# An encoder layer's projection: latents' squares and norms on ScalarE, three tiles reordered, the last tile's squares on GpSimd

## The reference

```python
hn = rms_norm(x, p['norm_attn'])
proj = einsum('bsd,de->bse', hn, p['w_in'])
gq, gk, gv, c_q, c_kv, k_pe = split(proj)      # 512, 128, 128, 256, 128, 32 columns
qa, ka = rms_norm per head of gq, gk; then rotated
qb = einsum(rms_norm(c_q), mla_w_uq)           # 8 heads of 64 + 32, each part rms-normed
kvb = einsum(rms_norm(c_kv), mla_w_ukv)        # 8 heads of 64 keys (rms-normed) + 64 values
k_pe = rotated(rms_norm(k_pe))
```

## Time and profile before

| | us |
|---|---|
| median of 3 runs | 1106.34 (1104.49 to 1106.6) |
| the profiled execution | 1105.62 |
| its span, first to last instruction | 1103.8 |
| TensorE busy | 1065.9 (97% of the span) |
| VectorE busy | 882.6 (80%) |
| ScalarE busy | 763.9 (69%) |
| GpSimd busy | 314.1 (28%) |

### The profile page before, as it was taken

How to read it: one execution, slowest core, us unless ns; L and a number is a source line. 1 busy time by engine, 2 the same in 40 slices (tenths; PEclk the granted TensorE clock), 3 DMA queues, 4 the chain that set the end, 5 groups by cost and what they waited for, 6 DMA issues and landing times.

```text
span 1103.8 us, 17117 instructions
## 1 busy us (share of the span) xinstructions
PE 1065.9 (97%) x5835; PEld 915.7 (83%) x5835; DVE 882.6 (80%) x1175; ACT 763.9 (69%) x1033; POOL 314.1 (28%) x346
## 2 busy tenths in 40 slices
PE   8989999999999999999599999999999999999996
PEld 7879978999889988887588888888888888888885
DVE  6787769888998853338898988989889898888982
ACT  8435458887887853443677777877778777787772
POOL 3475467021248602333311101111011110111011
PEclk9999999999999999999699999999999999999998
DMA  8132050010211328541699999999999999999982
GB/s 319 59 110 102 1 193 1 2 39 20 97 39 39 96 76 289 206 177 77 216 420 388 394 389 389 394 410 397 395 388 390 412 397 394 387 392 409 398 304 38
DMA packets 72816, 266.04 MB, mean 241 GB/s; under 512 B 6001, under 2 KB 8268, under 8 KB 72508
## 3 DMA queue, kind: packets, MB, share of 16 engines
q1 hardware_dynamic: 65376, 239.68, 55.6%
q0 software_dynamic: 7328, 25.68, 8.1%
q10 hardware_dynamic: 60, 0.01, 0.0%
HBM read 239.07 MB, written 26.28 MB: 240 GB/s over the span
## 4 chain that ended last, share of the span: by engine, by line
PE 49%; DVE 1%; DMA 1%; issue 0%; ACT 0%; POOLq 0%; POOL 0%; DVEq 0%; ACTq 0%
PE ps L1870 10%; PE ps L1872 10%; PE ps L1871 10%; PE ps L1886 5%; PE ps L1885 5%; PE ps L1884 5%; PE ps L1851 3%; DMA out<-y,give 1%; PE ps L1935 1%; DVE idx L1672 0%; DVE affT L1675 0%; DVE gates L1670 0%; ACT hi L1957 0%; DVE lo L2027 0%; POOLq L2107 0%
## 5 line engine op out<-in xcount | busy, mean ns | idle before, releaser
L2027 DVE TENSOR_TENSOR lo<-raw,hi 128x2048 fp32r<-128x2048 f32 x191 | 431.8, 2289 | 56.4 <-ACT hi L1957 56.0
L1957 ACT ACTIVATE hi<-raw 128x2048 fp32r<-128x2048 f32 x192 | 364.6, 1918 | 65.7 <-PE ps L1872 58.9
L1870 PE MATMUL ps<-hi,xehi 128*128 128x512 f32 x480 | 188.1, 392 | 0.2 <-DVE h L2039 0.2
L1872 PE MATMUL ps<-hi,xelo 128*128 128x512 f32 x480 | 186.8, 389 | 0.0
L1871 PE MATMUL ps<-lo,xehi 128*128 128x512 f32 x480 | 186.8, 389 | 0.0
L1806 POOL COPY take<-idxT 128x1 uint32 (+1 forms) x15 | 11.6, 775 | 357.7 <-PE ps L1851 357.7
L1870 PEld LDWEIGHTS ps<-hi,xehi 128*128 128x128 f32 x480 | 90.2, 188 | 18.8 <-issue 0.7
L1872 PEld LDWEIGHTS ps<-hi,xelo 128*128 128x128 f32 x480 | 90.1, 188 | 18.7
L1871 PEld LDWEIGHTS ps<-lo,xehi 128*128 128x128 f32 x480 | 90.2, 188 | 18.1
L1309 DVE TENSOR_TENSOR probTlo<-ps,probThi 128x512 fp32r<-128x512 f32 x128 | 87.8, 686 | 16.8 <-ACT probThi L1266 15.1
L1266 ACT ACTIVATE probThi<-ps 128x512 fp32r<-128x512 f32 x128 | 76.6, 599 | 33.9 <-PE ps L1148 33.9
(11 more groups left out here) (278 smaller groups left out, 2142.9 us busy)
## 6 DMA issues: line engine op xcount, KB each, us to landing
raw<-in_w_gate SPq DMA_DIRECT2D x64, 1024.0 KB, 7.8
raw<-in_w_up SPq DMA_DIRECT2D x64, 1024.0 KB, 7.6
raw<-in_w_down SPq DMA_DIRECT2D x64, 1024.0 KB, 8.1
w_raw<-in_w_in SPq DMA_DIRECT2D x8, 592.0 KB, 8.4
x<-in_x SPq DMA_DIRECT2D x8, 512.0 KB, 4.0
woraw<-in_w_o SPq DMA_DIRECT2D x4, 1024.0 KB, 5.0
o<-attention_out SPq DMA_DIRECT2D x8, 512.0 KB, 4.3
xr<-in_x SPq DMA_DIRECT2D x8, 512.0 KB, 6.5
```

The source lines that it names most:

```text
L1870: pe.matmul(ps[:, dst[n], :], rowhi[:, c, :], hi[w][:, cols], start=c == 0, stop=False)
L1872: last = pe.matmul(ps[:, dst[n], :], rowlo[:, c, :], hi[w][:, cols], start=False, stop=c == KD - 1)
L1957: act.activation(hi[s][:], raw[s][:], ACT.Copy).then_inc(hi_done, 1)
L2027: dve.tensor_tensor(lo[s][:], raw[s][:], hi[s][:].bitcast(F32), ALU.subtract).then_inc(lo_done, 1)
```

## The change

ScalarE's square of the latents becomes three, one per latent, scaled by one over the root of the column count and summed by the accumulator, so that they are means. VectorE's three sums and GpSimd's multiplication by the inverse counts go. The three latent norms move from VectorE to ScalarE as copies with a scale; `c_normed` and `stat_l` now count three for a tile, and the transposes wait for two of the norms.

ScalarE's order changes: x_square is no part of x_high. Between x_high(1) and the key weights stand now the first half of the query weights, latent_rows(0), the second half, x_square(1) and latent_norms(0). x_square(2) follows queries(0), later ones follow latents_high. latent_norms(t) stands ahead of latents_high(t). In VectorE's tile 2, latents_low(2) moves ahead of rotations(1).

In the last tile ScalarE makes copies only, and GpSimd multiplies them with themselves in `finish_rows`; VectorE's row_stats(7), query_stats(7) and key_stats(7) move to u = 5, 6 and 10, and row_roots(7) into `finish_rows`. TensorE's keys_values(7) waits for the copy of the queries alone.

```diff
--- before.py
+++ after.py
@@ -328,6 +328,7 @@
     half = UQ // 2
+    LATENTS = ((C_CQ, C_CKV), (C_CKV, C_KPE), (C_KPE, D_IN))
@@ -339,8 +340,8 @@
     xt_ready, xhi_done, xlo_done = sem("xt_ready"), sem("xhi_done"), sem("xlo_done")
-    lat_done, lat_squared, proj_done, row_copied, row_squared = (
-        sem(n) for n in ("lat_done", "lat_squared", "proj_done", "row_copied", "row_squared"))
+    lat_done, proj_done, row_copied, row_squared = (
+        sem(n) for n in ("lat_done", "proj_done", "row_copied", "row_squared"))
@@ -417,6 +418,7 @@
         def rotate_keys_pe(t):
...
             kpe = pj[:, t % TS, C_KPE:D_IN].rearrange("p (h c) -> p h c", h=1)
+            engine.wait_ge(c_normed, 3 * t + 3)
@@ -493,8 +495,9 @@
         def latent_roots(t):
-            pool.wait_ge(stat_l, t + 1)
-            mean(ssl, heads)
+            pool.wait_ge(stat_l, 3 * t + 3)
+            if t:
+                pool.wait_ge(c_normed, 3 * t)
...
         def row_roots(t):
@@ -524,8 +527,24 @@
                     x_root(t + 1)
-        row_roots(LAST)
-        return query_roots, key_roots, *row_pieces(pool, steps)
+        def last_row_squares():
+            qk = pj[:, LAST % TS, 0:C_V]
+            pool.wait_ge(row_copied, T)
+            pool.tensor_tensor(sq[:, 0:C_V], qk, qk, ALU.mult).then_inc(row_squared, 1)
+        def last_query_squares():
+            q = q_rows[:, LAST % TS].rearrange("p h c -> p (h c)")
+            pool.wait_ge(q_copied, 2 * T - 1)
+            pool.wait_ge(stat_b, LAST)
+            pool.tensor_tensor(sqq[:], q, q, ALU.mult).then_inc(q_copied, 1)
+        def last_key_squares():
+            keys = kv_rows[:, LAST % TS, 0:K_NOPE]
+            pool.wait_ge(kv_done, 3 * T - 1)
+            pool.wait_ge(stat_k, LAST)
+            pool.tensor_tensor(sqk[:], keys, keys, ALU.mult).then_inc(kv_done, 1)
+        return row_roots, (last_row_squares, last_query_squares, last_key_squares), query_roots, key_roots, *row_pieces(pool, steps)
...
     def tensor_program(pe):
@@ -547,7 +566,7 @@
         def latent_transposes(u):
-            pe.wait_ge(c_normed, u + 1)
+            pe.wait_ge(c_normed, 3 * u + 2)
@@ -571,7 +590,7 @@
         def keys_values(u):
...
-            pe.wait_ge(q_copied, 2 * (u + 1))
+            pe.wait_ge(q_copied, 2 * u + 1 if u == LAST else 2 * u + 2)
@@ -671,12 +690,11 @@
-        def split_up_weights():
+        def split_up_weights(i):
...
             act.wait_ge(gcol_ready, 1)
-            for i in range(2):
-                act.activation(w["uqhi"][:, i, :], uq_raw[:, i, :], ACT.Copy,
-                               scale=k["gcol"][:, G_QA + i:G_QA + i + 1]).then_inc(whi_done, 1)
+            act.activation(w["uqhi"][:, i, :], uq_raw[:, i, :], ACT.Copy,
+                           scale=k["gcol"][:, G_QA + i:G_QA + i + 1]).then_inc(whi_done, 1)
...
         def split_key_weights():
@@ -689,29 +707,39 @@
                                ACT.Copy).then_inc(xhi_done, 1)
-            if t:
-                x_square(t)
...
         def x_square(t):
...
                 act.wait_ge(stat_a, t - 1)
-                act.wait_ge(stat_l, t)
+            if t:
+                act.wait_ge(stat_l, 3 * t)
...
         def latent_rows(t):
...
             act.wait_ge(rx_done, t + 1)
-            act.wait_ge(ssx_done, max(2, t + 1))
-            act.wait_ge(stat_l, t)
+            act.wait_ge(ssx_done, t + 1)
...
             act.wait_ge(lat_copied, t + 1)
-            act.activation(sq[:, C_CQ:D_IN], pj[:, t % TS, C_CQ:D_IN], ACT.Square).then_inc(lat_squared, 1)
+            if t:
+                act.wait_ge(rl_done, t)
+                act.wait_ge(stat_l, 3 * t)
+            for i, (lo, up) in enumerate(LATENTS):
+                act.activation(sq[:, lo:up], pj[:, t % TS, lo:up], ACT.Square, scale=float(up - lo) ** -0.5,
+                               accum_out=ssl[:, i:i + 1]).then_inc(stat_l, 1)
+        def latent_norms(t):
+            act.wait_ge(rl_done, t + 1)
+            act.wait_ge(stat_l, 3 * t + 3)
+            for i, (lo, up) in enumerate(LATENTS):
+                row = pj[:, t % TS, lo:up]
+                act.activation(row, row, ACT.Copy, scale=rsl[:, i:i + 1]).then_inc(c_normed, 1)
...
         def latents_high(u):
@@ -725,6 +753,8 @@
                            ps[:, 6:8, 0:half], ACT.Copy).then_inc(q_copied, 1)
+            if u == LAST:
+                return
@@ -735,6 +765,8 @@
             act.activation(pj[:, t % TS, 0:C_CQ], row_ps, ACT.Copy, scale=rx[:, t:t + 1]).then_inc(row_copied, 1)
+            if t == LAST:
+                return
@@ -742,9 +774,10 @@
             value = u_ps.rearrange("p (h c) -> p h c", h=MH)[:, :, NOPE:NOPE + VD]
-            if u:
+            if u and u < LAST:
                 act.wait_ge(stat_k, u)
-            act.activation(sqk[:].rearrange("p (h c) -> p h c", h=MH), nope, ACT.Square).then_inc(kv_done, 1)
+            if u < LAST:
+                act.activation(sqk[:].rearrange("p (h c) -> p h c", h=MH), nope, ACT.Square).then_inc(kv_done, 1)
@@ -757,8 +790,11 @@
         x_high(1)
-        split_up_weights()
+        split_up_weights(0)
         latent_rows(0)
+        split_up_weights(1)
+        x_square(1)
+        latent_norms(0)
@@ -768,12 +804,16 @@
                 queries(0)
+                x_square(2)
...
                     x_high(t + 1)
+            latent_norms(t)
             latents_high(t)
+            if 1 < t < LAST:
+                x_square(t + 1)
@@ -838,21 +878,6 @@
-        def latent_stats(t):
-            dve.wait_ge(lat_squared, t + 1)
-            steps.did(dve.tensor_reduce(ssl[:, 0:1], sq[:, C_CQ:C_CKV], AX.X, ALU.add))
-            steps.did(dve.tensor_reduce(ssl[:, 1:2], sq[:, C_CKV:C_KPE], AX.X, ALU.add))
-            dve.tensor_reduce(ssl[:, 2:3], sq[:, C_KPE:D_IN], AX.X, ALU.add).then_inc(stat_l, 1)
-        def latent_norms(t):
-            row = pj[:, t % TS, :]
-            dve.wait_ge(rl_done, t + 1)
-            steps.did(dve.tensor_scalar(row[:, C_CKV:C_KPE], row[:, C_CKV:C_KPE], rsl[:, 1:2], None, ALU.mult))
-            dve.tensor_scalar(row[:, C_CQ:C_CKV], row[:, C_CQ:C_CKV], rsl[:, 0:1], None, ALU.mult).then_inc(c_normed, 1)
-            steps.did(dve.tensor_scalar(row[:, C_KPE:D_IN], row[:, C_KPE:D_IN], rsl[:, 2:3], None, ALU.mult))
         def row_stats(t):
@@ -873,7 +898,7 @@
         def key_stats(u):
...
-            dve.wait_ge(kv_done, 3 * u + 1)
+            dve.wait_ge(kv_done, 3 * u + 3 if u == LAST else 3 * u + 1)
...
         def mla_norms(u):
@@ -886,20 +911,17 @@
         split_up_weights()
-        latent_stats(0)
...
         row_stats(0)
-        latent_norms(0)
...
                 query_stats(1)
-                latent_stats(2)
...
                 row_norms(1)
-                latent_norms(2)
                 x_low(3)
+                latents_low(2)
@@ -908,10 +930,7 @@
                 x_low(2)
-            if t != 2:
-                latent_stats(t)
             if t == 1:
-                latent_norms(1)
@@ -920,10 +939,9 @@
                 key_stats(t - 1)
-                latent_norms(t)
...
                     x_low(t + 1)
-            if t > 1:
+            if t > 2:
@@ -1039,15 +1057,20 @@
-    def gpsimd_program(pool, query_roots, key_roots, row_norms, rotate_keys_pe, rotate_queries, rotate_keys, mla_parts):
+    def gpsimd_program(pool, row_roots, last_squares, query_roots, key_roots, row_norms, rotate_keys_pe, rotate_queries, rotate_keys, mla_parts):
...
         def finish_rows():
...
+            row_squares, query_squares, key_squares = last_squares
+            row_squares()
+            query_squares()
...
                 part()
+            key_squares()
+            row_roots(LAST)
@@ -1155,7 +1178,7 @@
                 if g == 0:
-                    pe.wait_ge(kv_done, 3 * T)
+                    pe.wait_ge(kv_done, 3 * T - 1)
@@ -1300,7 +1323,6 @@
         prepare("q", 0)
-        row_stats(LAST)
@@ -1326,9 +1348,11 @@
             if u == 5:
+                row_stats(LAST)
+            elif u == 6:
...
                 query_stats(LAST)
-            elif u == 7:
+            elif u == 10:
...
             if u == NU - 1:
```

## The result

| | before | after |
|---|---|---|
| median of 5 runs, us | 1106.34 (1104.49 to 1106.9) | 1111.17 (1110.84 to 1111.64) |
| the profiled execution, us | 1105.62 | 1111.63 |
| its span, us | 1103.8 | 1109.8 |
| TensorE busy, us | 1065.9 | 1067.2 |
| VectorE busy, us | 882.6 | 873.0 |

The ratio is 1.0047, with a 95% interval of 1.0036 to 1.0057: **slower by about 5 us**, at the forecast 1111.2. Ten microseconds of work did move from VectorE to ScalarE; the time went the other way.

A forecast was written before the change was run, and what follows sets the result against it. TensorE was taken to bound the kernel, with winnable gaps only in the first tiles and the seam. +2.6 us for chains and seam plus 2.3 for the clock gave +4.9, profiled 1110.5, median 1111.2, range 1107.0 to 1113.5.

The forecast's parts named there:

- The chain to queries(0): Tile 0: serial chain through ScalarE, GpSimd and VectorE takes 12.5 us from 22.4, so queries(0) starts at 34.9, 3.8 later.
- The pow of three columns: GpSimd's latents' roots at tile 0: taken as 0.85 us, not 1.71, since VectorE is idle then.
- The rival of growing stalls: Two-input VectorE work meets GpSimd's roots, 0.86 at tile 0 and again at tile 3, with the dip: 1113.0; 6%.
- Tile 1: Transposes wait 2.5 us for ScalarE's norms behind keys_values(0), starting at 46.5, 6.3 later than before.
- The step behind queries(0): TensorE's clock dips to half pace after the 4.7 us idle near 34.9, priced at 2.3 us (0 to 3.1).
- a dip shows nowhere before 520: Argument for the rival that the clock holds with the same chain: +2.6, 1109.0; 28%.
- passed at the full 2.4 GHz: Old trace's 2.78 us gap before queries(2) kept full clock; the 4.7 us idle is longer than any that did.
- Tile 2: The 0.61 gap before the transposes and the 2.78 before queries(2) go; queries(2) at 67.5, 2.8 later than before.
- Tile 3: Transposes could start at 82.0 but wait for norms until 82.4: a new stall of 0.4, 3.2 later than before.
- the rival of the shorter chain: Low bounds of squares and norms, no stall at tile 3: +1.2 or less, 1107.5; 11%, including 3% for no effect.
- The seam: Between projection and attention: the 0.68 at keys_values(7) goes, row_stats moves; nothing to 1.2 us earlier, 0.6 taken.
- The sum: 3.2 late at tile 3 less 0.6 at the seam, +2.6, plus 2.3 for the clock: +4.9, predicted 1111.2.

The follow-up runs named there:

- the first kernel of experiment 2: The changed kernel with VectorE's first tables ahead of split_key_weights and row_stats(0): 1109.76 us, ratio to before 1.003.
- the filled gap: The changed kernel with unread matmuls in TensorE's two long waits, 20 ahead of queries(0), 9 ahead of tile 1's transposes: 1108.33 us, ratio to before 1.0013.
- 2's second kernel: The changed kernel with GpSimd's latent_roots(0) ahead of x_root(1), ScalarE's norms and key weights ahead of x_square(1): 1109.73 us, ratio to before 1.0039.
- 4: The changed kernel with GpSimd's latents' roots of tile 3 ahead of its query roots: 1110.41 us, ratio to before 1.0043.
- experiment 5: The kernel before with VectorE's latents_low(2) ahead of rotations(1), nothing else: 1106.31 us, ratio to before 1.000.

## Why the prediction was right, and where it was not

**The chain to queries(0)** was right: 12.70 us from the copy at 22.51 to 35.21, where the sum gave 12.5, and the links stand at their prices (squares 0.93 for 0.92, norms 0.92 for 0.93). The experiments took two groups of its links away one by one, 1.7 and 1.5 us.

**The pow of three columns** took 0.86 at 27.32 while VectorE was idle, as taken, and not the 1.71 that it took beside VectorE's split. The Trainium skill, SBUF — State Buffer, section Who interferes with whom, has such a pair of instructions contend, and the two lengths agree with it. Short products on VectorE beside the pow did not lengthen it: 0.86 at 27.51 in the first kernel of experiment 2, where the last four products of the tables run from 27.16 to 27.79. The rival of growing stalls did not come about.

**Tile 1**: the wait was 2.35 for 2.5, with the cause named (ScalarE's norms start at 48.00 behind the three copies of keys_values(0)).

**The clock.** The step behind queries(0) was right: 2.1 for 2.3, shown by the filled gap. In all four profiles with a gap of 4.39 to 4.71 the clock fell within it, and from queries(0) to keys_values(0) 1.5, 2.1, 2.4 and 2.5 us were lost, so the price, too, varies between executions. The Trainium skill, TensorE: Matmul & The Clock Gate, section Why this matters for your kernels, has a long idle gap return the clock to half, and these four agree. But the step that **"a dip shows nowhere before 520", and 2.78 "passed at the full 2.4 GHz"**, took one execution for a rule. Gaps of 2.35 to 2.92 go either way here: behind 2.35 the clock fell in the profile of after and of 2's first kernel and not in those of 2's second kernel and of 4; at tile 2 of the kernels with the old tile 2 it kept up behind 2.78 and 2.80 and fell behind 2.79; and it fell behind 2.80 in 2's first kernel and 2.92 in experiment 5. The same gap with both outcomes shows that its length does not decide alone; what does is open. So the second fall, 1.5 us, was missing from the sum for after, and an expected part of one was missing from the kernel before.

**Tile 2**: both gaps went, as forecast. **Tile 3**: 0.75 for 0.4, the mechanism right (roots of the latents behind the query roots on GpSimd) and the size a third of a microsecond short, made up of hundredths in each link (6.27 for 6.2 in the row and query roots, 1.22 for 1.13, 0.86 for 0.8). The prediction's own working has a slip here: 65.2 is where its `clo` starts, and the 74.2 is added from 65.7, where `clo` ends. From 65.2 there would be no stall. The trace has the rotations where the sum had them, 1.5 behind the transposes (69.53 and 68.01). A second slip changes little: the rival of the shorter chain comes to +1.4 by its own terms, not +1.2.

**The seam** failed. The step was "row_stats moves into VectorE's fully booked first units as it leaves room ahead of them", with 0.6 taken. The room was an idle of VectorE that nobody could use before the first scores came; a reduction in it cost nothing, and in a booked stretch it costs its 0.73. The net was 0 (0.68 won, 0.7 given back). That GpSimd's three products cost TensorE nothing was right.

**The sum** came out at 1111.2 with errors that cancelled in part: against the forecast +4.9 the profiles differ by +6.0, from +1.5 (second fall), +0.35 (tile 3) and +0.6 (seam), less the 1.4 by which the routing was shorter in that execution; and the profiled executions lie 0.7 below the median of before and 0.5 above that of after. The mechanism is shown by the experiments; that the number was met to 0.1 is partly luck.

## What to carry to other kernels

Moving work to a less busy engine pays only if the new places in its queue are right: here a kernel with the same moves lost 5 us in one order and won 8 in another (how much of the 8 the new orders would give without the moves was not tested). So lay out each round trip between engines, put its links ahead of what nobody waits for, and move small steps into idle time that is certain, not into a booked stretch. A wait of TensorE costs its length and, by the clock, up to half of it again or more (1.5 to 2.5 us on 4.39 to 4.71, and at times 1.3 to 1.6 on 2.35 to 2.92); if it cannot be removed, idle products in it are a cheap test of that, and even a gain.

## What was not expected of the hardware

- The granted clock fell behind five of the nine gaps of 2.35 to 2.92 us in the projection of these profiles, at the same gap in one profile and not in another, for 1.3 to 1.6 us each time, and once (at 50 in the kernel after) more than a microsecond after TensorE had begun to work again.
- Filling a 2.8 us wait with 13 useless products made the kernel before faster by 0.14% [0.05%, 0.23%].
- The time of an execution goes with its mean granted clock: 1105.6 us on average at 0.990 or more, 1107.3 at 0.987 or less, in 64 executions of one kernel.
- GpSimd's products of two SBUF tensors took 1.25 us for 640 columns, 1.47 for 768 and 1.04 for 512 in the attention's first units, and TensorE waited for none of them.
